# A diffusion backbone on one core: router product in four column groups, fewer position and index products, one index for gather and scatter, third expert set early, 258-column transform

## The reference

```
def _fourier_mixer(h, w_out):
    hg = h.reshape(B, L, 4, 256)                                  # 4 channel groups of 256
    z = fft.fftn(hg, axes=(1, 3), norm='ortho').real.reshape(B, L, D_MODEL)
    return einsum('bld,de->ble', z, w_out)

def _hier_moe(h, ...):                                            # t: 384 tokens x 1024
    pg = softmax(t @ w_rg + b_rg)                                 # 4 groups: the best one, gi
    el = (t @ w_re + b_re).reshape(T, 4, 4)                       # 16 experts: the best two inside gi
    tv, ti = top_k(softmax(el[gi]), 2); tv = tv / sum(tv)
    gates = one_hot(gi * 4 + ti) * pg[gi] * tv
    hid = silu(t @ w_gate[e]) * (t @ w_up[e])                     # 1024 -> 512
    y = sum over e of gates[e] * (hid @ w_down[e])                # 512 -> 1024
```

## Time and profile before

| | us |
|---|---|
| median of 3 runs | 1116.37 |
| the runs | 1115.34, 1116.37, 1123.04 |
| the profiled execution | 1114.05 |
| its span, first to last instruction | 1112.3 |

### The profile page before, as it was taken

The page is one execution under the profiler, slowest core; times in us unless marked ns, Lnnn a source line. Parts: engine busy times, 40 slices in busy tenths (PEclk is TensorE's granted clock), DMA queues, the critical chain, the costliest instruction groups (busy, mean ns, idle before and its releaser), DMA issues.

```text
span 1112.3 us, 17281 instructions
## 1 busy us (share of the span) xinstructions
PE 936.5 (84%) x6715; PEld 517.7 (47%) x6716; DVE 224.4 (20%) x539; ACT 249.0 (22%) x451; POOL 171.6 (15%) x287
## 2 busy tenths in 40 slices
PE   2799999998999966998899995699949999887850
PEld 0355446654446453554455552364435555443420
DVE  1100355101544350000000101501330000000005
ACT  1111223221224031222222221420322222211112
POOL 2001002201001032121121120210212122111112
PEclk9899999998999977999999998799969999989995
DMA  9975464556442746999999965950436999999954
GB/s 380 315 285 224 153 228 153 199 227 229 151 149 95 309 171 262 418 423 419 420 417 425 418 264 205 411 233 18 178 109 254 418 375 418 418 425 422 419 221 167
DMA packets 68459, 317.68 MB, mean 286 GB/s; under 512 B 13252, under 2 KB 15588, under 8 KB 53184
## 3 DMA queue, kind: packets, MB, share of 16 engines
q1 hardware_dynamic: 54592, 290.68, 65.3%
q0 software_dynamic: 9856, 18.51, 4.7%
q10 hardware_dynamic: 3968, 7.87, 2.0%
HBM read 308.62 MB, written 17.38 MB: 293 GB/s over the span
## 4 chain that ended last, share of the span: by engine, by line
PE 39%; DMA 20%; DVE 5%; issue 2%; SPq 2%; ACT 1%; POOLq 0%; POOL 0%; DVEq 0%; ACTq 0%
PE ps L849 13%; DMA ring<-in_moe_w_down 10%; PE ps L856 9%; PE ps L745 7%; DMA deep<-in_moe_w_down 6%; DMA deep<-hrow,gi 2%; PE ps L766 2%; SPq L376 2%; PE ps L825 1%; PE ps L782 1%; PE ps L543 1%; DMA deep<-yrows 1%; DMA yrows<-deep,si 1%; DVE deep L1421 1%; PE ps L818 1%
## 5 line engine op out<-in xcount | busy, mean ns | idle before, releaser
L849 PE MATMUL ps<-ring,deep 128*64 128x256 f32 x1600 | 181.8, 384 | 14.4 <-DMA ring<-in_moe_w_up 10.4
L849 PEld LDWEIGHTS ps<-ring,deep 128*64 128x64 f32 x1600 | 118.9, 139 | 83.8 <-issue 14.8
L567 PE MATMUL ps<-deep,ring 128*128 128x384 f32 x384 | 129.2, 494 | 4.2 <-ACT deep L940 4.2
L1417 DVE TENSOR_TENSOR deep<-deep,ps 128x128 f32<-128x128 f32 x76 | 18.4, 284 | 439.3 <-PE ps L849 439.3
L856 PE MATMUL ps<-ring,deep 128*64 128x512 f32 x400 | 96.4, 626 | 8.3 <-DVE deep L1421 8.3
L567 PEld LDWEIGHTS ps<-deep,ring 128*128 128x128 f32 x384 | 72.7, 192 | 58.3 <-issue 10.1
L849 PE MATMUL ps<-deep 128*64 128x256 f32 x832 | 92.8, 379 | 3.9 <-DMA deep<-in_moe_w_up 3.4
L570 PE MATMUL ps<-ring,deep 128*128 128x512 f32 x192 | 87.9, 610 | 0.0
L745 PE MATMUL ps<-ring,deep 128*128 128x512 f32 x192 | 83.8, 594 | 1.4 <-ACT deep L1020 0.8
L849 PEld LDWEIGHTS ps<-deep 128*64 128x64 f32 x832 | 61.2, 137 | 39.0 <-issue 6.8
L501 PE MATMUL ps<-ring,scond 128*32 128x512 f32 x384 | 50.7, 649 | 21.8 <-DMA ring<-in_w_mod 21.0
(11 more groups left out here) (163 smaller groups left out, 809.2 us busy)
## 6 DMA issues: line engine op xcount, KB each, us to landing
ring<-in_w_mod SPq DMA_DIRECT2D x24, 2048.0 KB, 12.0
ring<-in_moe_w_gate SPq DMA_DIRECT2D x22, 2048.0 KB, 22.9
ring<-in_moe_w_up SPq DMA_DIRECT2D x22, 2048.0 KB, 27.7
ring<-in_moe_w_down SPq DMA_DIRECT2D x22, 2048.0 KB, 32.8
ring<-in_hgrn_w_in SPq DMA_DIRECT2D x10, 2048.0 KB, 8.6
deep<-in_moe_w_gate SPq DMA_DIRECT2D x10, 2048.0 KB, 20.6
deep<-in_moe_w_up SPq DMA_DIRECT2D x10, 2048.0 KB, 25.0
deep<-in_moe_w_down SPq DMA_DIRECT2D x10, 2048.0 KB, 30.7
```

The source lines that it names most:

```text
L567: last = mm(bank[:, 0:T], W[:, k, b * P:(b + 1) * P], hT[:, k, :], start=(k == 0), stop=(k == KD - 1))
L849: last = mm(ps[g * SLOTS:(g + 1) * SLOTS, GU_BANK[j], 0:2 * P], xt[:, b, h * SLOTS:(h + 1) * SLOTS], slot3(S[j])[:, k, g * F // 2:(g + 1) ...
```

## The change

- The router product of chunk k goes to column group k mod 4 (PSUM partitions 0, 32, 64, 96); two chunks accumulate in each. `lgT` takes all 128 partitions, and the three transposes become products with `stack`, a 0/1 matrix that adds the four groups.
- `both` (the sum of the two one-hot masks) gets a fourth tile of zeros and its own memory. One product with `upper` covers all tiles and the count, and one product with `ones` per tile adds that tile to all later ones.
- The rows of h are written to DRAM twice each, so that gather and scatter use one row number (4 x token + 2 x choice + half). The one-hot values, the index products and the index store have 96 columns and not 192.
- VectorE: several small instructions become one with broadcast operands; `pos_oh` and `vals` are made per choice c; the window counts (`over`, `npass`) are made behind them.
- GpSimd waits for `npass_set` before it loads the first window count, and for `idx_ready` and `hrow_out` only inside `gather`.
- SyncE's third set: its gate matrix goes to slot 8 when xn is turned, the other two when `hrow_out` is full. `idx_ready` and `gathered` are no longer waited for. Slots 6 and 8 change places.
- The channel transform makes 2 x 129 columns. The odd chunks read U one column later and use the positive sine table; the rows of `fourier_w_out` that belong to them are reversed before the launch.

```diff
@@ -300,7 +303,7 @@
             place(phase, u, mod_slot(u) if phase == "mod" else u % 2)
-        MOE_SLOTS = [[3, 4, 5, 0, 1, 2, 6, 7, 8], [4, 5, 3, 0, 1, 2, 6, 7, 8]]
+        MOE_SLOTS = [[3, 4, 5, 0, 1, 2, 8, 7, 6], [4, 5, 3, 0, 1, 2, 8, 7, 6]]
@@ -377,9 +380,9 @@
                     if u == 6:
-                        sp.wait_ge(M[l]["idx_ready"], 1)
+                        sp.wait_ge(n_tp, 6 * NORM[f"m{l}"] + 6)
+                    elif u == 7:
                         sp.wait_ge(M[l]["hrow_out"], 16 * TT)
-                        sp.wait_ge(M[l]["gathered"], 16)
@@ -540,7 +543,8 @@
                     pe.wait_ge(n_hA if k % 2 == 0 else n_hV, 8 * NORM[name] + 4 * part + k // 2 + 1)
-                    last = mm(ps[0:NL, 2, cols], wroute[:, l, k, :], hT[:, k, cols], start=(k == 0), stop=(k == KD - 1))
+                    g = SMALL * (k % 4)
+                    last = mm(ps[g:g + NL, 2, cols], wroute[:, l, k, :], hT[:, k, cols], start=(k < 4), stop=(k >= 4))
@@ -763,7 +767,7 @@
                         for k in range(2):
-                            last = mm(ps[:, 4 + n % 4, :], hT[:, 2 * g + k, t * P:(t + 1) * P], dft_c[:, k, :],
+                            last = mm(ps[:, 4 + n % 4, 0:2 * FOLD], hT[:, 2 * g + k, t * P:(t + 1) * P], dft_c[:, k, :],
@@ -788,7 +794,7 @@
                 for t in range(TT):
-                    last = pe.transpose(ps[:, 3, t * 32:t * 32 + NL], lgT[0:NL, t * P:(t + 1) * P], ident[0:NL, 0:NL])
+                    last = mm(ps[:, 3, t * 32:t * 32 + NL], lgT[:, t * P:(t + 1) * P], c_("stack"), start=True, stop=True)
@@ -802,21 +808,18 @@
                 pe.wait_ge(m["chosen"], 1)
+                pe.wait_ge(both_zero, 1)
+                mm(ps[:, 2, 0:(TT + 1) * NE], c_("upper"), both[:].rearrange("p t n -> p (t n)"), start=True, stop=False)
                 for t in range(TT):
-                    mm(ps[:, 2, t * NE:(t + 1) * NE], c_("upper"), both[:, t, :], start=True, stop=(t == 0))
-                    for b in range(t):
-                        mm(ps[:, 2, t * NE:(t + 1) * NE], c_("ones"), both[:, b, :], start=False, stop=(b == t - 1))
-                for t in range(TT):
-                    last = mm(ps[:, 2, TT * NE:(TT + 1) * NE], c_("ones"), both[:, t, :],
-                              start=(t == 0), stop=(t == TT - 1))
+                    last = mm(ps[:, 2, (t + 1) * NE:(TT + 1) * NE].rearrange("p (t n) -> p t n", n=NE), c_("ones"),
+                              both[:, t:t + 1, :].to_broadcast((P, TT - t, NE)), start=False, stop=(t == TT - 1))
...
                     for t in range(TT):
-                        last = mm(ps[:, 3, 0:2 * NE * WIN], pos_oh[:, c, t, :],
-                                  vals[:, c, t].rearrange("p v e w -> p (v e w)"),
+                        last = mm(ps[:, 3, 0:NE * WIN], pos_oh[:, c, t, :], vals[:, c, t].rearrange("p e w -> p (e w)"),
@@ -1067,8 +1070,8 @@
                     act.wait_ge(m["back_act"], 2 * t + 2)
-                    act.dma_start(scratch["hrow"][l].rearrange("(t p) n -> p t n", p=P)[:, t, :], hrow[:, t, :]
-                                  ).then_inc(m["hrow_out"], 16)
+                    act.dma_start(scratch["hrow"][l].rearrange("(t p) c n -> p t c n", p=P)[:, t],
+                                  hrow[:, t:t + 1, :].to_broadcast((P, 2, D))).then_inc(m["hrow_out"], 16)
@@ -1329,12 +1332,9 @@
                 step(V.tensor_scalar(ohg[:], ohg[:], -1.0, NEG, ALU.add, ALU.mult))
-                for t in range(TT):
-                    ins = V.tensor_tensor(el[:, t].rearrange("p (g e) -> p g e", g=NG),
-                                          lg[:, t, NG:NL].rearrange("p (g e) -> p g e", g=NG),
-                                          ohg[:, t].rearrange("p (g o) -> p g o", o=1).to_broadcast((P, NG, 4)),
-                                          ALU.add)
-                step(ins)
+                step(V.tensor_tensor(el[:].rearrange("p t (g e) -> p t g e", g=NG),
+                                     lg[:, :, NG:NL].rearrange("p t (g e) -> p t g e", g=NG),
+                                     ohg[:].unsqueeze(3).to_broadcast((P, TT, NG, 4)), ALU.add))
@@ -1345,45 +1345,42 @@
                 count_ = ps[:, 2, TT * NE:(TT + 1) * NE]
-                for c in range(2):
-                    V.tensor_tensor(e2[:, c], ps[:, 2, 0:TT * NE].rearrange("p (t n) -> p t n", n=NE), oh[:, c], ALU.mult)
+                step(V.tensor_tensor(e2[:], ps[:, 2, 0:TT * NE].rearrange("p (o t n) -> p o t n", o=1, n=NE)
+                                     .to_broadcast((P, 2, TT, NE)), oh[:], ALU.mult))
                 above = c_("above").rearrange("p (o n) -> p o n", o=1)
-                step(V.tensor_tensor(over[:], count_.rearrange("p (e o) -> p e o", o=1).to_broadcast((P, NE, WIN)),
-                                     above.to_broadcast((P, NE, WIN)), ALU.is_gt))
-                V.tensor_reduce(npass_f[:], over[:], AX.X, ALU.add)
...
                                      above[:, :, 1:WIN].to_broadcast((P, 2 * TT, WIN - 1)), ALU.is_ge))
-                V.tensor_copy(npass[:], npass_f[:])
...
                                             op0=ALU.mult, op1=ALU.add))
+                V.tensor_tensor(wv[:].rearrange("p c t w -> p (c t) w"), wnd[:],
+                                c_("value").rearrange("p (t o) -> p t o", o=1).to_broadcast((P, ct, WIN)), ALU.mult
+                                ).then_inc(windows_set, 1)
                 for c in range(2):
-                    for v in range(2):
-                        a = CONST_AT["value"][0] + 3 * (2 * c + v)
-                        V.tensor_tensor(wv[:, c, :, v, :], wnd[:, TT * c:TT * (c + 1), :],
-                                        b3(const[:, a:a + 3], WIN), ALU.mult)
-                step(V.tensor_tensor(pos_oh[:].rearrange("p c t s -> p (c t) s"),
-                                     c_("iota").rearrange("p (o s) -> p o s", o=1).to_broadcast((P, ct, P)),
-                                     place_.rearrange("p (t o) -> p t o", o=1).to_broadcast((P, ct, P)), ALU.is_equal))
-                for c in range(2):
-                    for t in range(TT):
-                        for v in range(2):
-                            ins = V.tensor_tensor(vals[:, c, t, v], oh[:, c, t].rearrange("p (e o) -> p e o", o=1)
-                                                  .to_broadcast((P, NE, WIN)),
-                                                  wv[:, c, t, v:v + 1, :].to_broadcast((P, NE, WIN)), ALU.mult)
-                    ins.then_inc(m["onehots"], 1)
+                    V.tensor_tensor(pos_oh[:, c], c_("iota").rearrange("p (o s) -> p o s", o=1).to_broadcast((P, TT, P)),
+                                    place_[:, TT * c:TT * (c + 1)].rearrange("p (t o) -> p t o", o=1).to_broadcast((P, TT, P)),
+                                    ALU.is_equal)
+                    if c == 0:
+                        dve.wait_ge(windows_set, l + 1)
+                    V.tensor_tensor(vals[:, c], oh[:, c].unsqueeze(3).to_broadcast((P, TT, NE, WIN)),
+                                    wv[:, c].rearrange("p t (o w) -> p t o w", o=1).to_broadcast((P, TT, NE, WIN)), ALU.mult
+                                    ).then_inc(m["onehots"], 1)
+                step(V.tensor_tensor(over[:], count_.rearrange("p (e o) -> p e o", o=1).to_broadcast((P, NE, WIN)),
+                                     above.to_broadcast((P, NE, WIN)), ALU.is_gt))
+                step(V.tensor_reduce(npass_f[:], over[:], AX.X, ALU.add))
+                V.tensor_copy(npass[:], npass_f[:]).then_inc(npass_set, 1)
                 dve.wait_ge(m["idx_mm"], 1)
-                V.tensor_scalar(slots_idx[:, :, 0:NE * WIN], ps[:, 3, 0:2 * NE * WIN]
-                                .rearrange("p (v n) -> p v n", v=2), -1.0, c_("base"), ALU.mult, ALU.add).then_inc(m["idx_ready"], 1)
+                V.tensor_scalar(slots_idx[:, 0:NE * WIN], ps[:, 3, 0:NE * WIN], -1.0, c_("base"), ALU.mult, ALU.add
+                                ).then_inc(m["idx_ready"], 1)
@@ -1502,15 +1499,14 @@
                 send_rows()
-                pool.wait_ge(m["idx_ready"], 1)
-                pool.wait_ge(m["hrow_out"], 16 * TT)
+                pool.wait_ge(npass_set, l + 1)
@@ -1519,17 +1515,18 @@
                 def gather(k_, col):
-                    G_.tensor_copy(gi[:], slots_idx[:, 0, col]).then_inc(m["gi_set"], 1)
                     pool.wait_ge(m["idx_ready"], 1)
+                    G_.tensor_copy(gi[:], slots_idx[:, col]).then_inc(m["gi_set"], 1)
+                    pool.wait_ge(m["hrow_out"], 16 * TT)
                     pool.wait_ge(m["gi_set"], k_)
-                    G_.indirect_dma_start(out=xg, out_offset=None, in_=scratch["hrow"][l].rearrange("t (h n) -> (t h) n", h=2),
+                    G_.indirect_dma_start(out=xg, out_offset=None, in_=scratch["hrow"][l].rearrange("t c (h n) -> (t c h) n", h=2),
                                           in_offset=bass.IndirectOffsetOnAxis(ap=gi[:, 0:1], axis=0),
```

(11 more changed lines are left out.)

47 lines of the change are left out of this document (26 added, 21 removed).

## The result

| | us |
|---|---|
| changed kernel, median of 4 runs (lowest to highest) | 1107.56 (1104.64 to 1109.44) |
| kernel before, beside it, median of 4 | 1118.32 (1115.34 to 1123.04) |
| ratio, 95% interval | 0.9896 (0.9863 to 0.9929) |
| the profiled execution of the changed kernel | 1104.64 |

Faster by 1.0%, where 1.5% was forecast; 1107.56 lies just above the range of 1087 to 1106.

The account below looks back on a forecast made before the run. Each expert stage was taken to end a fixed distance after its first passes, with TensorE bounding the Fourier mixer. Terms -4.5 - 2.2 - 10.2 = -16.9 took 1114.05 to 1097.1, raised to 1098 us; range 1087 to 1106.

Parts of the forecast that it names:

- the date of h's rows: Before the first gather: doubled row writes behind other transfers, 6.3 MB at 420 GB/s, land about 412.8 and 820.
- if it waits for hrow long past 413: Sign of being wrong: the first gather still waiting long past 413 us for the rows of h.
- The collision: First gather starts together with 4.2 MB of third-set weights, so takes 8.6 us; before, it took 3.39 and 3.38.
- The transform: Fourier transform over channels with 258 columns for 512: -10.0 us, and -0.2 for the last evacuation.
- the level: Starting time: profiled 1114.05 us, median of three 1116.37; half of the 0.2% difference was put on top.
- The serial stretch: Router product to first gather in each layer: -8.3 us in layer 0, -7.4 in layer 1.
- The wait for the second gather: TensorE's wait in the expert stages was to go: 2.28 us in layer 0, 0.46 in layer 1.
- late rows of h: Rival: rows of h come 5 us later than the indices, expert stages give about nothing; 1105 us, chance 0.13.
- The fair gather: Rival: DMA engines take turns, so the first gather takes 3.4 us beside the weights; 1088 us, chance 0.20.
- the change does nothing: Rival: router stretch saved and given back, mixer bound elsewhere; chance 0.05.
- it is slower: Rival: doubled writes delay the hrow semaphore 23 us behind forecast in each layer; 1144 us, chance 0.04.
- the early third set is worth nothing: Expert stages: the third set is needed two passes later, and the fourth still waits for expert 0.

Follow-up runs that it names:

- e1: Changed kernel with all three matrices of the third weight set held back until indices, rows of h and first gather are there: 1094.72 us, ratio 0.9797.
- e5: Kernel before with only the 258-column channel transform: 1105.79 us, ratio 0.9889.
- e9: Changed kernel with GpSimd's six small column loads for the next norm issued ahead of the norm: 1103.66 us, ratio 0.9863.
- e7: Changed kernel with all three matrices of the third set released at the rows' receipt, without waiting for the first gather: 1101.77 us, ratio 0.9874.
- e8: Kernel before with the router stretch of the change alone; third set waits as before, transform has 512 columns: 1105.32 us, ratio 0.9881.
- e3: Changed kernel with the rows of h written once, the gather's index being the scatter's shifted right by one: 1099.81 us, ratio 0.9834.
- e2: Changed kernel with only the third set's gate matrix early, the other two behind the first gather: 1096.41 us, ratio 0.9810.
- e6: Changed kernel with rows of h written once and only the gate matrix early, the other two behind the first gather: 1095.81 us, ratio 0.9800.
- e4: Changed kernel with rows of h written once and the whole third set held back as before: 1095.24 us, ratio 0.9798.
- e10: Changed kernel with the six small column loads moved ahead and the whole third set held back: 1094.58 us, ratio 0.9775.

## Why the prediction was wrong in its size

**What failed.** The step that failed is the date of h's rows: they were to be there at 412.8 and 820, just as the indices, and the gather was issued 3.1 us later than that in both layers. The prediction had named this as a sign of being wrong ("if it waits for hrow long past 413"). The collision was overpriced at the same time, by 1.15 and 1.4 us, and so about a third of the miss doesn't show. The transform's first block, 1.5 us short, is the second step that failed. Besides, the kernel before ran at a median of 1118.32 beside the changed one, 3.4 us above the level from which the forecast starts (1098 + 16.9 = 1114.9). So of the 9.6 us between 1107.56 and 1098, 6.1 are gain that didn't come and 3.4 are the level; without the level the time would lie inside the range, with the mechanism no better.

**The serial stretch was right in layer 0.** With the set held back (e1) the gather goes 8.2 us earlier by distance, for a forecast of 8.3 (7.4 against e5, which has the same stretch as before). The parts show it: the stack in 0.84 us for 0.73, index products 2.85 for 2.5, index copy 0.24 us behind the store; the position products took 1.1 for 1.7, and that made up for the others, which is luck in the sum. In layer 1 it is 5.9 for 7.4: the index products took 2.85 us there as well, the position products 1.5 for 1.0, and the store came 4.8 earlier.

**The rows of h were sized too early.** The forecast had 6.3 MB at 420 GB/s and the receipt at 412.8, just as the indices. The volume was right, the rate was not: the stretches show 54, 366 and 360 GB/s. The receipt came at 417.14, or 415.1 on the clock of before. The gather then went 0.8 us behind it, in layer 1 1.5 us, for which I had nothing; before, the gather stood as far behind its index copy (0.88 and 1.53 us), so this is GpSimd's step from the last wait to the issue, whichever wait is last. Together the issue was 3.1 us late in layer 0, and as much in layer 1 (813.71 + 9.41 = 823.1 for 820.0). e9 shows that the `colmod` loads, with the gate matrix behind them, were the cause in layer 0: they stand in no term of mine. In layer 1, which has no such loads, the receipt came 1.7 us late (812.25 + 9.41 = 821.7 for 820). The third write takes 9.30 us there, and 6.1 with the gate matrix held back (e1, e7); but that matrix was in the forecast's volume, and why the volume took longer was not settled.

**The collision was there, and smaller than priced**: 7.45 and 7.19 us for 8.6. Since e1 has 3.29 and 3.50, it costs about 4. The wait for the second gather did go. So layer 0: -4.5 forecast, 3.1 late, 1.15 back from the collision, -2.5 measured. Layer 1: the same 3.1 against -2.2 and 1.4 back, less a first pass of 9.11 us for 8.58: nothing left. The last term is within the spread of that pass (8.45 to 10.07 us in layer 1 of the thirteen profiles).

**The transform** was -10.2; e5 has just that. In the changed kernel's profile its first block took 5.41 us for 3.75 in the other two, and so -8.7; there the granted clock was 0.68:

```profile
710.40:715.70 5.30, 5.30 (x16) 4.06 (x16) 0.00 (x0) 1.16 (x3) 0.00 (x0) 0.68 1.05 385
```

The block is as slow in seven of the thirteen profiles (e8's 23.1 with 512 columns is one). TensorE had been idle for 1.9 us ahead of those seven, and for 1.5 to 1.7 ahead of five of the six others; e7, with 1.85, has the fast block. So the longer wait and the slow block go together in all thirteen, but 1.85 and 1.91 us are too near each other to call it the cause, which isn't settled. The rows of before show the fast block only, so the slow one could not be read from them. The three terms' misses, 2.0 + 2.3 + 1.5 = 5.8 us, are the difference between the forecast's -16.9 and the -11.1 of the profile by distance; the medians give -10.8.

**Of the rivals** "late rows of h" (1105) was the nearest in time and in kind; its 5 us of lateness were 3.1, and the transform's 1.5 came on top. It deserved more than 0.13, since forecast and rival differed by the time of one transfer with unpriced issues around it. The fair gather is refuted: 7.1 to 9.3 us beside the weights, with or without a backlog ahead (e1's second, e3, e7), 3.3 to 3.5 alone (e1, e2). As the prediction read taking turns packet by packet, the rule of the Trainium skill that stood beside it ("DMA: Bandwidth & Descriptors", "Queues, rings and completion order"), it should have been near 3.4; no run here shows whether the rule fails or that reading of it. That the change does nothing, and that it is slower, is excluded by the ratio.

That the early third set is worth nothing held: no kernel that keeps it, or its gate matrix, is faster than those without it (e6 against e4: 0.9800 and 0.9798). What I didn't do with that sentence was to draw its consequence. By the prediction's own terms the version without it would have gained 8.3 + 7.4 + 10.2 = 25.9 us and not 16.9, so the step was priced at a loss of 9.0; the runs make it 11 to 13.

## What to carry over

A transfer that nobody needs yet is not free when the next thing on the critical path is a small transfer: start the large one behind the small one's landing. When a due time rests on megabytes over bandwidth, list every issue on every queue in that stretch, small-piece loads above all, and look at DMA share beside GB/s, for a high share with few GB/s names them. If two parts of a change save and the third costs by your own terms, price the change without the third. Take the level from as many runs as the gain needs: 3.4 us of it were enough to leave the range.

## What the hardware showed beyond what was expected

- With six loads of 4 KB in small pieces under way and a 2 MB matrix behind them, the DMA engines were 0.89 busy at 54 GB/s for 2 us; the loads without a matrix beside them took a share of 0.35 at 8 GB/s (before). A write of 1 MB issued 12.5 us after the first of them landed after 10.5 us, and after 5.8 with the loads moved away (e9).
- The first gather of 256 KB took 3.2 to 3.6 us where no weights ran (before, e1, e2, e4, e5, e6, e8, e10), and gathers took 7.1 to 9.3 beside weights, whether these had been issued 3.7 us before (e1's second, 9.28) or start with it (e3, 7.39).
- ScalarE's issue of a broadcast write took 0.52 to 0.87 us in the changed kernel, for 0.33 of the plain one. The write landed after 9.2 us (median of six), after 5.2 with no matrix ahead of it (e1), and the plain one of half the size, before, after 2.6.
- TensorE ran the index products at a granted clock of 0.50, 12 in 2.85 us, in both layers: halving the columns moved saved a third (2.85 for 4.18).
